# Two edits to a two-layer hybrid backbone: where the attention mixer's head sums stand, and how the delta-rule mixer masks its block doubling

## The reference, cut to what matters

```python
pr = jax.nn.softmax(s, axis=-1)
pr = pr[:, :, 0] - lam * pr[:, :, 1]
y = jnp.einsum('bhqk,bkhd->bhqd', pr, v)
...
def finish(y):
    return _norm(y, norm_g, rms=True) * (1.0 - lam_init)
```

## Time and profile before

| | |
|---|---|
| median of 3 runs | 1952.47 us (1951.45 to 1954.13) |
| the profiled execution | 1955.58 us, its span 1953.8 us |
| TensorE matmul busy | 1673.4 us, 86% of the span |
| VectorE, ScalarE, GpSimd busy | 56%, 31%, 6% |
| mean granted TensorE clock | 0.89 of full speed |
| doubling, direction 0, layers 0 and 1 | about 531 to 563 us and 1535 to 1567 us |
| doubling, direction 1, layers 0 and 1 | about 612 to 645 us and 1616 to 1645 us |
| end of the attention stage, layers 0 and 1 | 174.3 us and 1263.2 us |

### The profile page before, as it was taken

One profiled execution on the slowest core, in us unless ns is written; L12 is line 12 of the kernel. 1 busy time (PEld: TensorE's weight loads), 2 busy tenths in 40 slices (PEclk: granted clock), 3 DMA queues, 4 the chain that ended last, 5 costly groups with the idle time before them and its releaser, 6 DMA issues. The chain is left out here.

```text
span 1953.8 us, 29824 instructions
## 1 busy us (share of the span) xinstructions
PE 1673.4 (86%) x12348; PEld 1335.7 (68%) x12348; DVE 1093.9 (56%) x1832; ACT 612.6 (31%) x978; POOL 125.4 (6%) x136
## 2 busy tenths in 40 slices
PE   6998999588778797999989969899777688879986
PEld 4766776455578575888877756778643677669975
DVE  2384456975655454554442355736686745557655
ACT  4344323334121125222222253423334112143342
POOL 0000111100223000000000000000100412000000
PEclk8999999698688697999999979999887778779998
DMA  9310211363101114222222021212052001154441
GB/s 373 114 49 33 71 49 44 132 245 123 67 2 45 38 50 178 102 90 105 88 86 85 1 100 66 76 45 86 33 196 88 2 1 45 43 221 172 171 170 43
DMA packets 41173, 182.03 MB, mean 93 GB/s; under 512 B 4560, under 2 KB 5328, under 8 KB 33232
## 3 DMA queue, kind: packets, MB, share of 16 engines
q1 hardware_dynamic: 41040, 180.14, 25.5%
HBM read 179.07 MB, written 1.05 MB: 92 GB/s over the span
## 5 line engine op out<-in xcount | busy, mean ns | idle before, releaser
L232 PE MATMUL ps<-hr,wr 128*128 128x512 f32 (+1 forms) x704 | 240.5, 342 | 3.2 <-DVE wr L225 0.9
L233 PE MATMUL ps<-hr,wr 128*128 128x512 f32 (+1 forms) x704 | 237.9, 338 | 0.0
L234 PE MATMUL ps<-hr,wr 128*128 128x512 f32 (+1 forms) x704 | 237.7, 338 | 0.0
L232 PE MATMUL ps<-hr_in,wr_in 128*128 128x512 f32 (+1 forms) x544 | 222.7, 409 | 14.1 <-DVE wr_in L225 12.3
L233 PE MATMUL ps<-hr_in,wr_in 128*128 128x512 f32 (+1 forms) x544 | 211.0, 388 | 0.0
L234 PE MATMUL ps<-hr_in,wr_in 128*128 128x512 f32 (+1 forms) x544 | 210.3, 387 | 0.0
L225 DVE TENSOR_TENSOR wr<-pr,wr 128x2048 fp32r<-128x2048 f32 x42 | 96.3, 2292 | 129.2 <-ACT wr L221 122.4
L232 PEld LDWEIGHTS ps<-hr_in,wr_in 128*128 128x128 f32 x544 | 109.9, 202 | 64.3 <-issue 33.5
L232 PEld LDWEIGHTS ps<-hr,wr 128*128 128x128 f32 x704 | 134.9, 192 | 21.7 <-DVE wr L225 6.7
L234 PEld LDWEIGHTS ps<-hr,wr 128*128 128x128 f32 x704 | 134.8, 191 | 13.9
L233 PEld LDWEIGHTS ps<-hr,wr 128*128 128x128 f32 x704 | 134.8, 191 | 13.6
(11 more groups left out here) (437 smaller groups left out, 3039.3 us busy)
## 6 DMA issues: line engine op xcount, KB each, us to landing
mix<-in_w_in SPq DMA_DIRECT2D x68, 512.0 KB, 3.4
pr<-in_w_up SPq DMA_DIRECT2D x28, 1024.0 KB, 4.8
pr<-in_ada_w SPq DMA_DIRECT2D x44, 512.0 KB, 6.5
mix<-in_w_up SPq DMA_DIRECT2D x16, 1024.0 KB, 4.8
ring<-in_ada_w SPq DMA_DIRECT2D x28, 512.0 KB, 4.5
pr<-in_w_down SPq DMA_DIRECT2D x14, 1024.0 KB, 4.8
pr<-in_ada_w SPq DMA_DIRECT2D x8, 1024.0 KB, 15.6
work<-in_w_out SPq DMA_DIRECT2D x16, 512.0 KB, 3.8
```

The lines of the kernel that those rows point to most:

```text
L232: nc.tensor.matmul(out, sh, mh, start=first, stop=False)
L233: nc.tensor.matmul(out, sh, ml, start=False, stop=False)
L234: return nc.tensor.matmul(out, sl, mh, start=False, stop=last)
```

## The change

Part one, in the attention stage: the tail has eight turns instead of six, so the same 72 blocks are dealt over two turns more; the wait for `sq` and the head sums stand on TensorE behind the tail's turn 1; `inverse_rms` stands on ScalarE behind turn 2; and VectorE does the two last products ahead of the last tile's `leave_dve` and `low`.

Part two, in the delta-rule stage: `first(u)` reads the unmasked blocks of `NT` at every level, with no wait for GpSimd. GpSimd no longer forms masked copies. At the start of direction 0, and again behind the semaphore `q` in direction 1, it builds three masks of 64 columns from six additions (64 rows by 64 columns each), each followed by a wait for itself, in front of its gathering (L2210). VectorE, once per direction, waits for the masks, and puts the product into X by a `copy_predicated` (mask as int32, broadcast over the eight matrices of a tile) in place of the addition. What the unmasked product has outside the level's blocks is not copied.

```diff
-    HEAD, TAIL = 2, 6
+    HEAD, TAIL, SUMS_AFTER = 2, 8, 1
...
             for i in range(TAIL):
                 proj.pe_turn(pe, HEAD + 2 * (len(units) + 3) + i)
-            pe.wait_ge(S("sq"), 1)
-            head_sums(E, pe, sq, (6, 7), layer).then_inc(S("ss"), 1)
+                if i == SUMS_AFTER:
+                    pe.wait_ge(S("sq"), 1)
+                    head_sums(E, pe, sq, (6, 7), layer).then_inc(S("ss"), 1)
...
-            proj.leave_dve(dve, proj.end - 1)
-            proj.low(dve, proj.end + 1)
             dve.wait_ge(S("rn"), 1)
             link(nc.vector.tensor_tensor(two(y, layer), two(y, layer), two(sq, layer), ALU.mult))
             nc.vector.tensor_scalar(two(tiles(mix, 2, 2), layer), two(y, layer), par[:, Q_DN:Q_DN + 1], 1.0 - lam_init,
                                     ALU.mult, ALU.mult)
+            proj.leave_dve(dve, proj.end - 1)
+            proj.low(dve, proj.end + 1)
...
                 proj.act_turn(act, HEAD + 2 * (len(units) + 3) + i)
+                if i == SUMS_AFTER + 1:
+                    inverse_rms(E, S, act, (6, 7), sq, layer, 1.0 / HD, Q_EPS)
             proj.leave_act(act, proj.end - 1)
             proj.high(act, proj.end + 1)
-            inverse_rms(E, S, act, (6, 7), sq, layer, 1.0 / HD, Q_EPS)
...
+    masks = ct[:, T:T + (LEVELS - 1 - SOLVED) * P // 2]
...
-                    if u < NC:
-                        pe.wait_ge(S("ct"), NC * d + u + 1)
...
-                                mm = nc.tensor.matmul(out[rows_of(h)], mat(ct, u % 2, hd)[rows_of(h), rows_of(h)],
+                                mm = nc.tensor.matmul(out[rows_of(h)], mat(NT, j, hd)[rows_of(h), rows_of(h)],
                                                       small(j, 1, hd)[rows_of(h)], start=True, stop=True)
...
             for d in range(2):
                 if d:
+                    pool.wait_ge(S("q"), 1)
+                for n in range(LEVELS - 1 - SOLVED):
+                    for h in range(2):
+                        a, b = (c(C_LEVEL + (e * LEVELS + SOLVED + n) * P + h * HALF, HALF)[rows_of(h)] for e in range(2))
+                        nc.gpsimd.tensor_tensor(masks[rows_of(h), n * HALF:(n + 1) * HALF], a, b, ALU.add).then_inc(S("masks"), 1)
+                        pool.wait_ge(S("masks"), 2 * (LEVELS - 1 - SOLVED) * d + 2 * n + h + 1)
+                if d:
                     pool.wait_ge(S("x_up"), NU + TILES)
...
-                if d:
-                    pool.wait_ge(S("q"), 1)
-                for u, (l, j) in enumerate(units[:NC]):
-                    if u >= 2:
-                        pool.wait_ge(S("t1"), NU * d + u - 1)
-                    mask = c(C_LEVEL + (d * LEVELS + l) * P).rearrange("p (b t) -> p b t", b=1).to_broadcast([P, HEADS, P])
-                    nc.gpsimd.tensor_tensor(ct[:, (u % 2) * 512:(u % 2 + 1) * 512].rearrange("p (b t) -> p b t", b=HEADS),
-                                            four(NT, j).rearrange("p (b t) -> p b t", b=HEADS), mask, ALU.mult).then_inc(S("ct"), 1)
...
+                    if u == 0:
+                        dve.wait_ge(S("masks"), 2 * (LEVELS - 1 - SOLVED) * (d + 1))
                     if u < NC:
+                        mask = masks[:, (l - SOLVED) * HALF:(l - SOLVED + 1) * HALF].bitcast(I32).rearrange("p (m t) -> p m t", m=1)
                         dve.wait_ge(S("d_mm"), NU * d + u + 1)
-                        ins = nc.vector.tensor_tensor(four(X, j), four(X, j), bank[:, :], ALU.add)
+                        ins = nc.vector.copy_predicated(four(X, j).rearrange("p (m t) -> p m t", t=HALF), mask.to_broadcast([P, 2 * HEADS, HALF]),
+                                                        bank[:, :].rearrange("p (m t) -> p m t", t=HALF))
```

More of the change, by code:

```diff
@@ L1925, in rwkv @@
     with Stage(nc) as S, nc.Block() as block:
-        for n in ("link", "tT", "raw", "raw_out", "ct", "t1", "t1_out", "x_up", "d_mm", "u_mm", "s_mm", "u", "s"):
+        for n in ("link", "tT", "raw", "raw_out", "masks", "t1", "t1_out", "x_up", "d_mm", "u_mm", "s_mm", "u", "s"):
             S(n)
```

## The result

The changed kernel took 1942.92 us, median of 12 runs, against 1954.4 us for the kernel before (12 runs). The ratio is 0.9943, with a 95% interval from 0.9927 to 0.996, so 0.57% or some 11 us faster. The forecast was 1945.8 us. One of the twelve runs, of 2749.72 us, had a mean granted TensorE clock of 0.546; the ratio is taken without it, and the median of the other eleven is 1941.96 us.

A forecast was written before the change was run, and what follows sets the result against it. TensorE, busy 86% of the span, bounds the kernel, so its waits count. Direction 0 6.8, masks -1.6, direction 1 0.3, attention stage 1.2: 6.7 us gained, 1952.5 to 1945.8 us; range 1942.2 to 1951.0.

The forecast's parts named there:

- GpSimd makes VectorE late in direction 0: Doubling, direction 0: masked copies slow VectorE on TensorE's path; removing them gains 1.9 us to step 2, 0.8 at L2266, per layer.
- The first hole: Direction 0: TensorE's 3.87 us wait for ScalarE's copy L2507, delayed by VectorE's step 2, shrinks to 2.0 us.
- The clock through the shorter hole: Direction 0: after a 2.0 us TensorE wait the clock stays at its upper level; 0.8 us gained per layer, bounds 0 and 1.25.
- The whole of direction 0: Doubling, direction 0: VectorE's savings and the clock, less 0.1 us for predicated copies, gain 3.4 us per layer, 6.8 in two.
- The predicated copy at the addition's price: Doubling: predicated copy takes about 0.62 us start to start against the addition's 0.60; 0.1 us lost per layer in direction 0.
- The third rival: Doubling: predicated copy runs at half pace, 1.2 us start to start; change ends 5.9 us slower, 1958.4 us; chance 0.08.
- Direction 1: Doubling, direction 1: VectorE mostly reads PSUM there; layer 1 gains 0.3 us after the predicated copies, layer 0 nothing.
- The masks: Delta-rule stage start: GpSimd's six additions hold up VectorE's chain; 0.8 us lost per layer, 1.6 in all, bounds 0 and 2.3 per layer.
- The attention stage's end: Behind TensorE's last projection matmul: head sums moved earlier shorten the end by 1.6 us in layer 0, 0.5 in layer 1.
- The loop pays for the blocks it gives up: Attention loop: two more tail turns take three blocks out, adding waits; 0.5 us lost in layer 0, 0.4 in layer 1.
- the first rival: Most gain eaten by mask additions, loop waits or falling clock; any two leave 0.8 to 2.8 us gain; chance 0.27.

The follow-up runs named there:

- the two later comparisons: The unaltered changed kernel timed again twice against the kernel before, beside other variants: 0.9928 (1941.36 us) and 0.992 (1940.87 us).
- kernel with the copies kept: Changed kernel with GpSimd's 48 masked copies still made, into a tile nobody reads: 0.9987 to the kernel before, 1951.11 us.
- the deal by layer: Changed kernel with eight tail turns in layer 0 and six in layer 1: 0.9909 (1938.39 us), then 0.9912 (1941.35 us), to the kernel before.
- the deal alone: Kernel before with eight tail turns instead of six, head sums, roots and products still at the stage's end: 1.0013, 1956.57 against 1954.3 us.
- the later turns: Changed kernel, tail turns eight/six by layer, exponentials behind units 4, 5, 6, state turns behind 13, 14, 15: 0.9928 (1941.41 us), then 0.991 (1939.74 us).

## Why the prediction was right, and where it was not

The time fell in the range, 2.9 us below the forecast, and the direction was right. The size was too small, and that the time still fell in the range is in part luck: the median of the eleven runs, 1941.96, lies just below its lower end of 1942.2, and the same kernel gained 14 and 16 us by the ratios of the two later comparisons (0.9928 and 0.992), against 11 in the first and 6.7 forecast. By its steps:

- **GpSimd makes VectorE late in direction 0** (1.9 + 0.8 us a layer): right, to 0.1 us in each row that it names (L2247 and L2268, which it leaves out, lost 0.18 each as well). The first hole shrank by 2.0 us (1.9 predicted). The kernel with the copies kept shows the mechanism by itself.
- **The clock through the shorter hole** (0.8 us a layer): right in most cases, 1.00 behind 1.87 us. From L2256 to L2266 VectorE took 7.17 us instead of 7.88, so in that profile it gave some 0.7. It does not always hold: in one profile of three of the changed kernel in layer 0, and in another in layer 1, the clock fell 1.5 us behind this hole, and L2081 took 1.12 us behind the next.
- **The whole of direction 0**: from its first matmul to L2113 it took 40.8, 41.0, 40.2 and 41.3 us in layer 0 of the four profiles with the copies feeding TensorE, mean 40.8, and 36.3, 37.6, 37.8 and 37.4 in the changed kernel's three and part two's, mean 37.3: 3.5 us gained. In layer 1 it is 40.2 against 37.2: 3.0 us. Predicted 3.4 each. The two profiles of the deal by layer, whose direction 0 is the same code, have 36.6 and 36.5 in layer 0 and 38.4 and 38.3 in layer 1; with them it is 3.8 and 2.6. A difference of 1 us between two single profiles says nothing here.
- **The predicated copy at the addition's price**: right, 0.61 to 0.63 us from start to start against 0.60. The third rival, at 1.2 us, is out.
- **Direction 1** (0.3 us): fits, but is too small to tell. Layer 1 from first matmul to L2113 was 31.0 us (1613.62 to 1644.63) and is 30.7 (1603.10 to 1633.77), and the changed kernel's other two profiles have 30.5 and 29.7; layer 0 34.3 and 34.5.
- **The masks** (1.6 us lost): mis-sized. From the stage's first matmul to direction 0's it took 44.1 us before (484.28 to 528.37) and 44.2 after in layer 0, 41.1 and 41.9 in layer 1; the third profile of the changed kernel has 43.7 and 41.2. Over the nine profiles with the masks and the four without, the means differ by 0.1 us in layer 0 and 0.4 in layer 1: some 0.5 in all. The row that the bound came from the earlier trace rows has GpSimd instructions of over 1 us against VectorE's; here they are of 0.38 beside a VectorE chain without a gap, and it is GpSimd that takes longer. Which of the two differences decides it was not tested. The Trainium skill, page "SBUF — State Buffer", section "Who interferes with whom", says that the two lock each other out, and that the order of issue decides who waits. The trace agrees with the first (6.05 us for six instead of 2.30); no run here shows the order of issue. The 4.6 us that the prediction drew from the rule, one hold-up of VectorE for every addition, did not come. The section also excepts VectorE's 2-port modes from the rule that an instruction with one SBUF input does not meet GpSimd, which the prediction left out: the two of L2260, with one tensor in SBUF, take 0.87 us together without the copies and 1.15 beside the copies that were kept (there L2267). No run here shows which mode they are in.
- **The attention stage's end** (1.6 and 0.5 us): right, 1.59 and 0.51 by the gaps.
- **The loop pays for the blocks it gives up** (0.5 and 0.4 us lost): this step failed, in both layers. It said that "a block less is 0.7 us more of waiting". In layer 0 the new deal took the waits away, 3.4 us down to 0.3. It also changes which turn has two blocks and which has one: counted from the code, each pass now has two and then one, where before the order changed from pass to pass. Two of the four waits (0.64 and 0.30 us) stood behind a turn of one block, but the longer two (0.92 and 1.54) did not, so why those went is not shown. In layer 1 the deal made a wait of 3.05 us, with L225 of the turn last in a gapless row of VectorE's, and a stretch of lower clock behind it. Net the deal alone lost 2.3 us, with no change inside its interval, not far from the 0.9 predicted, but by two errors of opposite sign: 3.1 us gained in layer 0 instead of 0.5 lost, 3.9 lost in layer 1 instead of 0.4.
- **What the sum missed**: some 4.8 us in the first comparison, 7 and 9 by the ratios of the later ones. By the medians part one gave 1.8 more than predicted, part two 3.0 more, of which 1.1 is the masks (some 0.5 lost instead of 1.6). Of the rest one place was seen, a stage that the change doesn't touch: the second mixer's in layer 1 (153.3 instead of 156.1). It goes with the clock there, but its cause was not isolated. The rest stays open.
- **A sum of the first rival** is off: any two of its three terms leave 1.4 to 2.8 us of gain, not 0.8 to 2.8. Nothing else hangs on it.

## What to carry to other kernels

When GpSimd's work is hidden from TensorE, look at what it costs VectorE's instructions with two SBUF inputs; if VectorE is late on TensorE's path, taking GpSimd's work away pays. Shifting filler blocks out of a loop is not priced by their length: write down how many blocks stand ahead of each wait under the old and the new deal, and for each shape of the loop by itself. Where one program's stages differ by 3 us from run to run with the clock, and one stretch by 9, an edit worth 3 us is judged by its row, in several profiles, and can't be judged by the total. A stage's time is compared only where the stage opens at the same clock.

## What the runs showed of the hardware

- In the start of the delta-rule stage six short GpSimd instructions (0.38 us each alone) beside a gapless chain on VectorE took 6.05 us instead of 2.30, at 0.15 us for the whole VectorE chain. Longer ones (1.09 us alone), as in the kernel with the copies kept, held up VectorE: 2.06 instead of 1.21 us for one addition, though not for every one that they overlapped; the two of L2260, of 128x512 with one tensor in SBUF, took 1.15 instead of 0.87.
- A predicated copy of 128x512 from PSUM with a mask broadcast in runs of 64 columns takes 0.73 us, beside GpSimd too.
- Behind an idle time of 1.86 to 1.88 us in direction 0 TensorE's clock stayed at 2.4 GHz in ten of twelve cases (two layers in six profiles) and fell 1.5 us later in two; with the later turns it fell at an idle time of 1.88 us in two of four. Around one of 3.62 us it fell in all twelve. So in this kernel the length of the idle time alone did not settle the level.
